# The first norm's weights as one row, spread over the partitions by two products

## The chip, the cores and the metric

The kernel runs on one core of a Trainium2 chip. The metric is the device time of one execution in microseconds (us). The kernel before takes 1307.15 us, the median of three runs (1306.59 to 1307.22).

## The reference

A decoder trunk with four pre-norm layers over 256 tokens of width 1024, in float32. Each layer is a token mixer (latent attention, block-sparse attention, a state-space scan, latent attention again) and then a squared-ReLU MLP. What matters here is the very beginning: every mixer starts from `rmsnorm(x, norm_mix[i])`, and the first one multiplies that by `mla_w_in`.

```
def rmsnorm(x, g):
    y = x * rsqrt(mean(x * x, axis=-1) + 1e-6)
    return y * g                      # g: 1024 weights, the same for all tokens

for i in range(4):
    h = rmsnorm(x, norm_mix[i])
    x = x + mixer_i(h)                # i = 0: proj = h @ mla_w_in, ...
    x = x + sq_relu_mlp(rmsnorm(x, norm_mlp[i]), w1[i], w2[i])
return rmsnorm(x, norm_final)
```

## The kernel before, in words

Tokens lie on the 128 partitions, so the 256 tokens are two tiles, t = 0 and t = 1, each 128 x 1024. The kernel is written with explicit semaphores; each engine has one program, in a fixed order, and waits where it needs something.

**A norm, stage 0.** ScalarE squares a tile and sums each row (line 621). VectorE makes mean plus epsilon (`ms`, line 697), GpSimd raises it to the power -0.5 (`rstd`, line 781, in `pool_norm`), and VectorE multiplies `x * rstd * gbc` in two halves of 512 columns (line 703, in `dve_scale_x`). `gbc` is a 128 x 1024 tile that holds the 1024 weights of the norm on every partition. TensorE turns each half by four transposes against the identity `ident` (line 797, `pe_tr`), ScalarE copies the result out of PSUM as the high part of a split into two numbers (line 649), and VectorE makes the low part (line 725).

**Weights.** All weight matrices come in `units` of up to 1 MB, in order, through four slots of `raw`. SyncE issues their loads (line 2214) between loads of other things; ScalarE makes the high part `whi` (lines 565 and 566), VectorE the low part `wlo` (lines 579 and 582), and a slot's next load waits for that. Units 0 and 1 are the two halves of the first 512 columns of `mla_w_in`, and they are split in halves so that TensorE can start early. Unit 2 is loaded by two DMAs (the last 64 columns of `mla_w_in`, and a part of `mla_w_uq`), unit 3 is from `mla_w_ukv`.

**The order in stage 0.** ScalarE: squares of tile 0, high parts of tile 0, `whi` of unit 0, squares of tile 1, high parts of tile 1, `whi` of unit 1, then unit 2. VectorE: `ms`, `xn` and low parts of tile 0, `wlo` of unit 0, `ms` of tile 1, four small rotary operations (`dve_turns`), `xn` and low parts of tile 1, nine more small ones (`dve_angles`), `wlo` of unit 1. TensorE: transposes of tile 0, seven products of `ident` with itself that nobody reads (line 2314), unit 0 with tile 0, transposes of tile 1, unit 0 with tile 1, unit 1 with tile 0, the small bias product (line 1673), unit 1 with tile 1, and then the rest of latent attention.

**SyncE's queue at the start:** x tile 0 (line 2194), `gbc` (line 2192, function `gains`, a load that reads the one row of weights 128 times), `ident` (line 2196), unit 0, x tile 1 (line 2200), unit 1 and so on.

**GpSimd's program at the start:** small memsets, loads of `pos_i` and `invf`, the power for tile 0, then loads of `relx` and `onehot` (for the bias product), two of `qkvg` for the first latent attention (`latent_gains(0)`, lines 2239 and 2241; they are read by VectorE at line 1500), then the power for tile 1, then a wait for unit 1's load, `latent_gains(1)` and seven small loads for the state-space layer (lines 2259 and 2260). Then come the powers of the latents (line 1557) and the store of the bias rows (line 1682).

Of the kernel before, what the change touches and what calls it, by code (L numbers as in the profile page):

```python
# [17 lines left out]
ALU = mybir.AluOpType  # L18
# [3 lines left out]
P = 128  # L22
SEQ = 256
T = SEQ // P
# [79 lines left out]
def build(nc, A, out, stages):  # L104

    ctx = ExitStack()
    with ctx:
        def sb(name, shape, dt=F32, c=ctx):
            return c.enter_context(nc.sbuf_tensor(name, shape, dt))

        def sem(name):
            return ctx.enter_context(nc.semaphore(name))
# [10 lines left out]
        gbc = sb("gbc", [P, DM])  # L123
# [10 lines left out]
        acc = [[ctx.enter_context(nc.psum_tensor(f"acc{t}{h}", [P, 512], F32)) for h in range(2)] for t in range(T)]  # L134
# [11 lines left out]
        x_loaded = [sem(f"x_loaded{t}") for t in range(T)]  # L146
        x_ready = sem("x_ready")
        gain_loaded = sem("gain_loaded")
        ssq_done = sem("ssq_done")
        ms_done = sem("ms_done")  # L150
        rstd_done = sem("rstd_done")
        xn_done = sem("xn_done")
# [51 lines left out]
        with ExitStack() as stage:  # L204
            S_sb = sb("S_sb", [P, 2, 384], F32, stage)
            P_sb = sb("P_sb", [P, 2, 384], F32, stage)
            PT_sb = sb("PT_sb", [P, 2, 384], F32, stage)
            ohi = sb("ohi", [P, 2, 2, SEQ], F32R, stage)
            olo = sb("olo", [P, 2, 2, SEQ], F32R, stage)
            qT = sb("qT", [P, 2, 4, SEQ], F32, stage)  # L210
            kT = sb("kT", [P, 2, 4, SEQ], F32, stage)
            v_sb = sb("v_sb", [P, 2, T, 512], F32, stage)
            with ExitStack() as mla:
                chi = sb("chi", [P, 4, SEQ], F32R, mla)
                clo = sb("clo", [P, 4, SEQ], F32R, mla)
                kpT = sb("kpT", [P, SEQ], F32, mla)
                qpT = sb("qpT", [P, 2, 2, SEQ], F32, mla)

                relx = sb("relx", [BUCKETS + 1, MOBA_H], F32, mla)
                onehot = sb("onehot", [BUCKETS + 1, 384], F32, mla)  # L220
                biasrow = sb("biasrow", [MOBA_H, 384], F32, mla)
                pos_i = sb("pos_i", [P, T], I32, mla)
                pos_f = sb("pos_f", [P, T], F32, mla)
                invf = sb("invf", [P, ROPE // 2], F32, mla)
                ang = sb("ang", [P, 4, T, ROPE // 2], F32, mla)
            bias = sb("bias", [P, MOBA_H, 384], F32, stage)
# [451 lines left out]
        def dve_scale_half(dve, j, t, half):  # L678

            n = slice(512 * half, 512 * half + 512)  # L680
            if j:
                dve.wait_ge(x_ready, (j - 1) * 2 * T + 2 * t + half + 1)
            else:
                dve.wait_ge(x_loaded[t], 16)
            dve.wait_ge(gain_loaded, 16 * (j + 1))
            nc.vector.tensor_tensor(xn[:, t, n], x[:, t, n], gbc[:, n], ALU.mult).then_inc(xn_done, 1)

        def dve_scale_x(dve, j, t, meanwhile=lambda: None):

            c = j * T + t  # L690
            if deferred(j):
                dve_scale_half(dve, j, t, 0)
                dve_scale_half(dve, j, t, 1)
                return
            wait_x(dve, j, t)
            dve.wait_ge(ssq_done, c + 1)
            nc.vector.tensor_scalar(ms[:, c:c + 1], ssq[:, c:c + 1], 1.0 / DM, EPS, ALU.mult, ALU.add).then_inc(ms_done, 1)
            meanwhile()
            dve.wait_ge(gain_loaded, 16 * (j + 1))
            dve.wait_ge(rstd_done, norm_index[j] * T + t + 1)  # L700
            for half in range(2):
                n = slice(512 * half, 512 * half + 512)
                nc.vector.scalar_tensor_tensor(out=xn[:, t, n], in0=x[:, t, n], scalar=rstd[:, c:c + 1],
                                               in1=gbc[:, n], op0=ALU.mult, op1=ALU.mult).then_inc(xn_done, 1)

        def dve_gain_upper(dve, j, t):
            dve.wait_ge(gain_loaded, 16 * (j + 1))
            wait_x(dve, j, t)
            n = slice(512, 1024)
            nc.vector.tensor_tensor(xn[:, t, n], x[:, t, n], gbc[:, n], ALU.mult).then_inc(xg_done, 1)  # L710
# [253 lines left out]
        norm_index, n_full = {}, 0  # L964
# [1214 lines left out]
        @block.sync  # L2179
        def _(sp):  # L2180

            def gains(j):
                if j >= NN:
                    return
                if j:
                    sp.wait_ge(xn_done, 2 * j * T)
                if j == NN - 1:
                    src = A["norm_final"].unsqueeze(0)
                else:
                    kind, L, _ = stages[j]  # L2190
                    src = A["norm_mlp" if kind == "mlp" else "norm_mix"][L:L + 1, :]
                sp.dma_start(gbc[:], src.to_broadcast([P, DM])).then_inc(gain_loaded, 16)

            sp.dma_start(x[:, 0, :], A["x"][0, tok(0), :]).then_inc(x_loaded[0], 16)
            gains(0)
            sp.dma_start(ident[:], A["c_ident"]).then_inc(ident_loaded, 16)
            for n, (a, b, srcs) in enumerate(units):
                s, k = n % SLOTS, n // SLOTS
                if n == 1:
                    sp.dma_start(x[:, 1, :], A["x"][0, tok(1), :]).then_inc(x_loaded[1], 16)  # L2200
                if n == SLOTS:
                    sp.dma_start(mask[:], A["c_mask"]).then_inc(mask_loaded, 16)
                if n in stage_unit:
                    gains(stage_unit[n] + 1)
                if k:
                    sp.wait_ge(w_split[s], k)
                w = b // len(srcs)
                for i, src in enumerate(srcs):
                    if isinstance(src, tuple):
                        off, k_rows, width, src = src  # L2210
                        dst = raw[:, s, off:off + k_rows * width].rearrange("p (a b) -> p a b", a=k_rows)
                    else:
                        dst = raw[:, s, :a * b].rearrange("p (a b) -> p a b", a=a)[:, :, i * w:(i + 1) * w]
                    sp.dma_start(dst, src).then_inc(raw_loaded[s], 16)
            for t in range(T):
                for half in range(2):
                    if half:
                        sp.wait_ge(xn_upper_done, norm_index[NN - 1] * T + t - T + 1)
                    else:
                        sp.wait_ge(xn_done, 2 * ((NN - 1) * T + t + 1))  # L2220
                    n = slice(512 * half, 512 * half + 512)
                    sp.dma_start(out[0, t * P:(t + 1) * P, n], xn[:, t, n]).then_inc(out_stored, 16)
            sp.wait_ge(out_stored, 32 * T)

        @block.gpsimd
        def _(pool):
# [3 lines left out]
            pool.wait_ge(pool_const, 2)  # L2230
            nc.gpsimd.memset(ones[:], 1.0).then_inc(pool_const, 1)
            pool.wait_ge(pool_const, 3)
            pool.dma_start(pos_i[:], A["positions"].rearrange("o (t p) -> p (o t)", p=P),
                           allow_slow_non_contiguous=True).then_inc(rope_loaded, 16)
            pool.dma_start(invf[:], A["c_invfreq"].to_broadcast([P, ROPE // 2])).then_inc(rope_loaded, 16)
# [2 lines left out]
            def latent_gains(i):  # L2238
# [2 lines left out]
                pool.dma_start(qkvg[:, i, QR:QR + KVR],  # L2241
                               A["mla_kv_norm"][i:i + 1, :].to_broadcast([P, KVR])).then_inc(qkvg_loaded[i], 16)

            pool.dma_start(relx[0:BUCKETS, :], A["rel_bias"]).then_inc(rel_loaded, 16)
            pool.dma_start(onehot[:], A["c_onehot"]).then_inc(rel_loaded, 16)
            latent_gains(0)
            if 0 in norm_index:
                pool_norm(pool, 0, [1])
            pool.wait_ge(raw_loaded[1], raw_count[1])
            latent_gains(1)  # L2250
            if "ssd" in kinds:
# [54 lines left out]

        @block.tensor
        def _(te):
            te.wait_ge(ident_loaded, 16)
            if "moba" in kinds and not bias_in_mla:  # L2310
                pe_bias(te)
            pe_tr(te, 0, 0)
            for _ in range(7):
                nc.tensor.matmul(acc[0][0][:, 0:P], ident[:], ident[:], start=True, stop=True)
            for j, (kind, L, i) in enumerate(stages):
                if kind == "mlp":
                    pe_mlp(te, j, L)
                if kind == "ssd":
                    pe_ssd(te, j, L)
                if kind == "mla":  # L2320
                    pe_mla(te, j, L)
                if kind == "moba":
                    pe_moba(te, j, L)
                if j + 1 < len(stages) and not deferred(j + 1):
                    pe_tr(te, j + 1, 0)
# [20 lines left out]
```

## Time and profile before

| what | value |
|---|---|
| median of 3 runs | 1307.15 us (1306.59 to 1307.22) |
| the profiled execution, its own time | 1307.72 us |
| its span, first to last instruction | 1305.9 us |
| TensorE busy with products | 1279.3 us, 98% of the span |
| VectorE busy | 891.4 us, 68% |
| ScalarE busy | 672.6 us, 51% |
| GpSimd busy | 43.5 us, 3% |

How to read it: times are microseconds from the start of the span. PE is TensorE's products and PEld its weight loads, DVE is VectorE, ACT ScalarE, POOL GpSimd and SPq SyncE's queue. L703 is line 703 of the kernel. A float32 product with float32 operands shows as two records in the trace. The ends of TensorE's records are modelled, and they overlap, so the distance between starts is the pace.

### The profile page before, as it was taken

How to read it: one execution, taken by the hardware profiler on the slowest of the kernel's cores; microseconds unless marked ns; L12 is line 12 of the kernel's file. 1: busy time of each engine (PE TensorE's matmuls, PEld its weight loads, DVE VectorE, ACT ScalarE, POOL GpSimd, SP SyncE). 2: the span in 40 equal slices, each digit the busy share in tenths (PEclk: the TensorE clock that was granted, in tenths of full speed). 3: DMA queues.
4: the chain of work that ended last, by engine and by line, in shares of the span. 5: the costliest groups of instructions: out<-in, count | busy, mean ns of one | idle time of the engine just before them, and what ended most of it. 6: DMA issues, size and time to landing. Idle time of an engine off the chain costs nothing.

```text
span 1305.9 us, 18369 instructions
## 1 busy us (share of the span) xinstructions
PE 1279.3 (98%) x7578; PEld 1118.2 (86%) x7578; DVE 891.4 (68%) x1180; ACT 672.6 (51%) x861; POOL 43.5 (3%) x58
## 2 busy tenths in 40 slices
PE   6999999999999999999999999999999999999998
PEld 5888888888999888887999888888887888888886
DVE  5877666665666666666899886766667876666664
ACT  5555554444555554444776654544445646454442
POOL 3000000000000000000101110000000000000000
PEclk9999999999999999999999999999999999999999
DMA  8754466555845375555574643755554334565540
GB/s 287 145 171 147 144 228 207 193 193 162 233 148 184 131 257 193 193 166 161 176 229 136 199 155 124 246 193 193 191 182 141 116 132 130 166 237 193 193 162 33
DMA packets 146067, 230.93 MB, mean 177 GB/s; under 512 B 7683, under 2 KB 112429, under 8 KB 145984
## 3 DMA queue, kind: packets, MB, share of 16 engines
q1 hardware_dynamic: 143136, 221.66, 51.0%
q0 software_dynamic: 2848, 8.10, 2.9%
q8 instruction: 61, 1.00, 0.3%
q14 instruction: 22, 0.18, 0.0%
HBM read 227.08 MB, written 2.65 MB: 176 GB/s over the span
## 4 chain that ended last, share of the span: by engine, by line
PE 83%; DVE 13%; DMA 1%; issue 1%; ACT 1%; POOL 1%; SPq 0%; POOLq 0%; DVEq 0%; ACTq 0%
PE bank L981 16%; PE acc L903 12%; PE acc L904 12%; PE acc L907 12%; PE bank L985 8%; PE bank L599 5%; PE bank L601 5%; PE bank L600 5%; DVE wlo L582 5%; DVE cacc L1961 2%; PE bank L1413 1%; PE bank L1116 1%; PE bank L797 1%; PE bank L1419 1%; PE bank L1101 1%
## 5 line engine op out<-in xcount | busy, mean ns | idle before, releaser
L582 DVE TENSOR_TENSOR wlo<-raw,whi 128x2048 fp32r<-128x2048 f32 (+2 forms) x207 | 464.8, 2255 | 139.9 <-ACT whi L566 139.8
L566 ACT ACTIVATE whi<-raw 128x2048 fp32r<-128x2048 f32 (+2 forms) x207 | 387.2, 1882 | 46.3 <-PE acc L907 44.1
L981 PE MATMUL bank<-hsplit,whi 128*128 128x512 f32 x896 | 219.1, 389 | 0.0
L904 PE MATMUL acc<-wlo,uhi 128*128 128x512 f32 x512 | 200.1, 391 | 0.0
L903 PE MATMUL acc<-whi,uhi 128*128 128x512 f32 x512 | 200.0, 391 | 0.0
L981 PEld LDWEIGHTS bank<-hsplit,whi 128*128 128x128 f32 x896 | 168.2, 188 | 34.8
L907 PE MATMUL acc<-whi,ulo 128*128 128x512 f32 x512 | 159.2, 390 | 0.0
L599 PE MATMUL bank<-hsplit,whi 128*128 128x256 f32 (+2 forms) x540 | 154.0, 285 | 0.5 <-DVE xn L1991 0.5
L601 PE MATMUL bank<-hsplit,wlo 128*128 128x256 f32 (+2 forms) x540 | 150.9, 279 | 0.0
L600 PE MATMUL bank<-hsplit,whi 128*128 128x256 f32 (+2 forms) x540 | 150.8, 279 | 0.0
L1038 ACT ACTIVATE relu<-bank 128x512 f32<-128x512 f32 x56 | 33.5, 598 | 183.8 <-PE bank L985 183.8
L985 PE MATMUL bank<-hsplit,wlo 128*128 128x256 f32 x896 | 120.3, 277 | 0.0
L985 PEld LDWEIGHTS bank<-hsplit,wlo 128*128 128x128 f32 x896 | 114.3, 188 | 4.7
L907 PEld LDWEIGHTS acc<-whi,ulo 128*128 128x128 f32 x512 | 96.1, 188 | 20.4
L903 PEld LDWEIGHTS acc<-whi,uhi 128*128 128x128 f32 x512 | 96.1, 188 | 18.6
L904 PEld LDWEIGHTS acc<-wlo,uhi 128*128 128x128 f32 x512 | 96.1, 188 | 18.2
L599 PEld LDWEIGHTS bank<-hsplit,whi 128*128 128x128 f32 (+2 forms) x540 | 100.7, 186 | 1.8 <-issue 1.4
L600 PEld LDWEIGHTS bank<-hsplit,whi 128*128 128x128 f32 (+2 forms) x540 | 101.0, 187 | 0.9 <-issue 0.7
L601 PEld LDWEIGHTS bank<-hsplit,wlo 128*128 128x128 f32 (+2 forms) x540 | 101.2, 187 | 0.0
L1059 DVE TENSOR_TENSOR relu<-bank,relu 128x512 f32<-128x512 f32 x56 | 38.7, 691 | 91.1 <-ACT relu L1038 91.1
L1043 ACT ACTIVATE uhi<-rsq 128x512 fp32r<-128x512 f32 x64 | 40.6, 634 | 111.2 <-DVE rsq L1061 82.2
L1064 DVE TENSOR_TENSOR ulo<-rsq,uhi 128x512 fp32r<-128x512 f32 x64 | 44.3, 692 | 47.7 <-ACT uhi L1043 47.7
(252 smaller groups left out, 1811.9 us busy)
## 6 DMA issues: line engine op xcount, KB each, us to landing
raw<-in_mlp_w SPq DMA_DIRECT2D x128, 1024.0 KB, 5.5
raw<-in_ssd_w_in SPq DMA_DIRECT2D x18, 1024.0 KB, 5.4
raw<-in_mla_w_o SPq DMA_DIRECT2D x16, 1024.0 KB, 4.9
raw<-in_mla_w_ukv SPq DMA_DIRECT2D x8, 1024.0 KB, 6.0
raw<-in_moba_w_qkv SPq DMA_DIRECT2D x16, 512.0 KB, 5.4
raw<-in_ssd_w_out SPq DMA_DIRECT2D x8, 1024.0 KB, 5.6
raw<-in_mla_w_uq SPq DMA_DIRECT2D x8, 768.0 KB, 5.8
raw<-in_mla_w_in SPq DMA_DIRECT2D x4, 1024.0 KB, 7.4
```

What stands on the lines that cost most here:

```text
L566: nc.scalar.activation(high[:, lo:e], raw[:, s, lo:e], ACT.Copy).then_inc(w_hi_done[s], 1)
L582: nc.vector.tensor_tensor(low[:, lo:e], raw[:, s, lo:e], high[:, lo:e].bitcast(F32), ALU.subtract).then_inc(w_split[s], 1)
L599: nc.tensor.matmul(ps, lhs[0], rhs[0], start=start, stop=False)
L600: nc.tensor.matmul(ps, lhs[0], rhs[1], start=False, stop=False)
L601: return nc.tensor.matmul(ps, lhs[1], rhs[0], start=False, stop=stop)
L903: nc.tensor.matmul(acc[t][half][:], lh, wh[:, k, n], start=begin and k == 0, stop=False)
L904: nc.tensor.matmul(acc[t][half][:], lh, wl[:, k, n], start=False, stop=False)
L907: mm = nc.tensor.matmul(acc[t][half][:], ll, wh[:, k, n], start=False, stop=end and k == 1)
L981: nc.tensor.matmul(ps, w[0][:, k, m * P:(m + 1) * P], hsplit[:, k].rearrange("p a n -> p (a n)"), start=k == 0, stop=False)
L985: return nc.tensor.matmul(ps[:, 0:SEQ], w[1][:, k, m * P:(m + 1) * P], hsplit[:, k, 0, :], start=False, stop=k == KD - 1)
L1043: nc.scalar.activation(uhi[:, c % 2].rearrange("p a b -> p (a b)"), rsq[:, c % 2, :], ACT.Copy).then_inc(uhi_done, 1)
L1064: nc.vector.tensor_tensor(ulo[:, c % 2].rearrange("p a b -> p (a b)"), rsq[:, c % 2, :], uhi[:, c % 2].rearrange("p a b -> p (a b)").bitca ...
```

## The change

One row of weights (4 KB) is loaded into partition 0 of `gbc` instead of the copy for all 128 partitions. GpSimd sets 128 ones in partition 0 of a buffer that is free then. TensorE multiplies the column of ones (1 x 128) with each half of the row (1 x 512), which leaves the weights on every partition in the two PSUM tiles `acc[1][0]` and `acc[1][1]`; VectorE reads them from there in line 703, for both tiles. All later norms load `gbc` as before; their counts are one load lower. In GpSimd's program the power of tile 1 moves ahead of the loads of `relx`, `onehot` and the first pair of `qkvg`.

```diff
+            ones_row = S_sb[0:1, 0, 0:P]
@@ dve_scale_x
-            dve.wait_ge(gain_loaded, 16 * (j + 1))
+            if j:
+                dve.wait_ge(gain_loaded, 16 * j)
+            else:
+                dve.wait_ge(gains_spread, 1)
             dve.wait_ge(rstd_done, norm_index[j] * T + t + 1)
             for half in range(2):
                 n = slice(512 * half, 512 * half + 512)
                 nc.vector.scalar_tensor_tensor(out=xn[:, t, n], in0=x[:, t, n], scalar=rstd[:, c:c + 1],
-                                               in1=gbc[:, n], op0=ALU.mult, op1=ALU.mult).then_inc(xn_done, 1)
+                                               in1=gbc[:, n] if j else acc[1][half][:], op0=ALU.mult,
+                                               op1=ALU.mult).then_inc(xn_done, 1)
@@ SyncE
             sp.dma_start(x[:, 0, :], A["x"][0, tok(0), :]).then_inc(x_loaded[0], 16)
-            gains(0)
+            sp.dma_start(gbc[0:1, :], A["norm_mix"][0:1, :]).then_inc(gain_row_loaded, 16)
             sp.dma_start(ident[:], A["c_ident"]).then_inc(ident_loaded, 16)
@@ GpSimd
             nc.gpsimd.memset(ones[:], 1.0).then_inc(pool_const, 1)
             pool.wait_ge(pool_const, 3)
+            nc.gpsimd.memset(ones_row, 1.0).then_inc(ones_row_set, 1)
             pool.dma_start(pos_i[:], ...
...
+            if 0 in norm_index:
+                pool_norm(pool, 0, [1])
             pool.dma_start(relx[0:BUCKETS, :], A["rel_bias"]).then_inc(rel_loaded, 16)
             pool.dma_start(onehot[:], A["c_onehot"]).then_inc(rel_loaded, 16)
             latent_gains(0)
-            if 0 in norm_index:
-                pool_norm(pool, 0, [1])
             pool.wait_ge(raw_loaded[1], raw_count[1])
             latent_gains(1)
@@ TensorE
+            te.wait_ge(ones_row_set, 1)
+            te.wait_ge(gain_row_loaded, 16)
+            for half in range(2):
+                mm = nc.tensor.matmul(acc[1][half][:], ones_row, gbc[0:1, 512 * half:512 * half + 512], start=True, stop=True)
+            mm.then_inc(gains_spread, 1)
             te.wait_ge(ident_loaded, 16)
```

## Rows read from the trace of the kernel before

**Rows 1.** The page's chain that ended last: shares of the span by engine.

```profile
PE 83%; DVE 13%; DMA 1%; issue 1%; ACT 1%; POOL 1%; SPq 0%; POOLq 0%; DVEq 0%; ACTq 0%
```

**Rows 2.** The same chain in order, first 30 us: start, length, what.

```profile
2.12 9.68 DMA raw<-in_mla_w_in
...
11.82 1.07 ACT whi L565
...
12.91 1.23 DVE wlo L579
14.14 1.03 DVE wlo L582
...
19.32 0.47 PE bank L599
...
25.03 0.75 PE bank L1673 x2
...
26.28 2.27 DVE wlo L582
```

**Rows 3.** Timeline of tile 0: start, length, engine, line, [idle before, releaser].

```profile
0.75 0.38 SPq L2194 DMA_DIRECT2D x<-in_x  x1
1.19 0.42 SPq L2192 DMA_DIRECT2D gbc<-in_norm_mix  x1
...
4.89 1.06 ACT L621 ACTIVATE junk<-x 128x1024 f32<-128x1024 f32 x1 [2.87 <-DMA x<-in_x]
...
7.06 1.41 DVE L703 SCALAR_TENSOR_TENSOR xn<-x,rstd,gbc 128x512 f32<-128x512 f32 x2 [0.75 <-POOL rstd L781]
...
7.96 1.94 PE L797 MATMUL bank<-ident,xn 128*128 128x128 f32 x8 [7.96 <-DVE xn L703]
...
9.69 2.86 PE L2314 MATMUL acc<-ident 128*128 128x128 f32 x14
...
9.93 0.60 ACT L649 ACTIVATE hsplit<-bank 128x512 fp32r<-128x512 f32 x1 [0.26 <-PE bank L797]
...
11.82 1.06 ACT L565 ACTIVATE whi<-raw 128x1024 fp32r<-128x1024 f32 x1 [1.29 <-DMA raw<-in_mla_w_in]
```

**Rows 4.** DMA issues of the first 40 us: issues, KB, median us from issue to landing.

```profile
x<-in_x SPq DMA_DIRECT2D x2, 512.0 KB, 7.7
...
gbc<-in_norm_mix SPq DMA_DIRECT2D x1, 512.0 KB, 5.1
...
qkvg<-in_mla_kv_norm POOLq DMA_DIRECT2D x2, 128.0 KB, 6.8
...
ident<-in_c_ident SPq DMA_DIRECT2D x1, 64.0 KB, 5.0
...
onehot<-in_c_onehot POOLq DMA_DIRECT2D x1, 49.5 KB, 5.6
...
drow<-in_ssd_d POOLq DMA_DIRECT2D x1, 0.1 KB, 3.4
```

**Rows 5.** TensorE's records of line 2314: duration ns min, median, max.

```profile
L2314 PE MATMUL acc<-ident x14: 275/421/422, 9.7 to 12.3; 128*128 128x128 f32 x14
```

**Rows 6.** Windows: busy us (records) of PE, PEld, DVE, ACT, POOL; granted clock, DMA share, GB/s.

```profile
5.00:10.00 5.00, 2.04 (x10) 2.07 (x11) 1.86 (x4) 1.71 (x4) 2.75 (x5) 1.00 0.94 295
```

**Rows 7.** Timeline of tile 1's norm and GpSimd's next loads, same columns as rows 3.

```profile
15.45 0.56 POOL L781 TENSOR_TENSOR rstd<-ms,neghalf 128x1 f32<-128x1 f32 x1 [6.31 <-DVE ms L697]
...
16.36 1.41 DVE L703 SCALAR_TENSOR_TENSOR xn<-x,rstd,gbc 128x512 f32<-128x512 f32 x2
...
17.86 1.26 ACT L649 ACTIVATE hsplit<-bank 128x512 fp32r<-128x512 f32 x2 [2.75 <-PE bank L797]
...
19.31 0.58 POOL L2239 DMA_DIRECT2D qkvg<-in_mla_q_norm  x1 [3.29 <-DMA raw<-in_mla_w_in]
```

**Rows 8.** VectorE by line and shape: count, busy us, mean ns, idle before.

```profile
L957 DVE SCALAR_TENSOR_TENSOR x<-acc,rstd,x 128x512 f32<-128x512 f32 x16 | 11.4, 746 | 6.0 <-PE acc L907 6.0
...
L703 DVE SCALAR_TENSOR_TENSOR xn<-x,rstd,gbc 128x512 f32<-128x512 f32 x4 | 2.8, 748 | 0.8 <-POOL rstd L781 0.8
```

More of the change, by code:

```diff
@@ L148, in build @@
         gain_loaded = sem("gain_loaded")
+        gain_row_loaded = sem("gain_row_loaded")
+        ones_row_set = sem("ones_row_set")
+        gains_spread = sem("gains_spread")
         ssq_done = sem("ssq_done")
@@ L698, in dve_scale_x @@
             meanwhile()
-            dve.wait_ge(gain_loaded, 16 * (j + 1))
+            if j:
+                dve.wait_ge(gain_loaded, 16 * j)
+            else:
+                dve.wait_ge(gains_spread, 1)
             dve.wait_ge(rstd_done, norm_index[j] * T + t + 1)
@@ L703, in dve_scale_x @@
                 nc.vector.scalar_tensor_tensor(out=xn[:, t, n], in0=x[:, t, n], scalar=rstd[:, c:c + 1],
-                                               in1=gbc[:, n], op0=ALU.mult, op1=ALU.mult).then_inc(xn_done, 1)
+                                               in1=gbc[:, n] if j else acc[1][half][:], op0=ALU.mult,
+                                               op1=ALU.mult).then_inc(xn_done, 1)
         def dve_gain_upper(dve, j, t):
-            dve.wait_ge(gain_loaded, 16 * (j + 1))
+            dve.wait_ge(gain_loaded, 16 * j)
             wait_x(dve, j, t)
@@ L2184, in gains @@
                     return
-                if j:
-                    sp.wait_ge(xn_done, 2 * j * T)
+                sp.wait_ge(xn_done, 2 * j * T)
                 if j == NN - 1:
```

## The prediction

> **What bounds the kernel now.** I read the page's chain first. It lies on TensorE for 83% of the span and on VectorE for 13%, with only 1% on DMA [rows 1]. So the change can touch only the start, and what it moves there is kept or lost once. The chain in order of time shows the start [rows 2]: until 11.80 us it is the load of weight unit 0 (issued 2.12, 9.68 us long), then ScalarE's high parts at 11.82, VectorE's low parts at 12.91 and 14.14, then tile 1's norm, and TensorE from 19.32 nearly without a pause to the bias product at 25.03. None of the later steps waits for a load in this chain. If `whi` of unit 0 starts D earlier, all of this moves by D, and behind it the kernel is bound by engines and keeps it.
>
> The timeline of tile 0 shows the second strand [rows 3]. x lands before 4.89, `xn` starts at 7.06, the transposes at 7.96, ScalarE's last high part at 9.93, and it ends at 10.53. ScalarE then idles 1.29 us for unit 0. Tile 0's norm therefore has a slack of 1.29 us, and this is the most that loads alone can give unless tile 0 gets faster too.
>
> **The load that goes.** `gbc` lands at 1.19 + 5.1 = 6.3 us, x at 4.85, both of 512 KB and one behind the other in one queue [rows 3, 4]. The copy thus holds the queue back some 6.3 - 4.9 = 1.4 us. Unit 0 should land at 11.8 - 1.4 = 10.4. The GpSimd loads that move away from 7 to 9 us are 50 + 128 + 128 KB, about 0.3 MB; at 295 GB/s [rows 6] that is another 1.0 us at most. Unit 0 lands between 9.4 and 10.4, which is at or ahead of ScalarE's 10.53. Weights stop being the late one, and tile 0 decides.
>
> **What is put into tile 0's strand.** `xn` used to wait for `rstd` at 7.06. It now waits also for two products, and these for the row. Three terms:
>
> 1. The row's landing. It is issued behind x at 1.19. If it stays behind x it lands just after 4.85; I take 4.9. The bounds: the smallest load of the stretch took 3.4 us (0.1 KB, another queue), so 4.6; `ident`, issued third and 64 KB, took 5.0, so 6.2 [rows 3, 4].
> 2. The products, 4 x 128 columns each in float32. Line 2314 shows seven of 128 columns in 2.86 us, 0.41 us each [rows 3], so 4 x 0.41 = 1.63 us for one of 512 and 3.3 for two. The upper limit goes by the slow records alone: they overlap by half of 421 ns [rows 5], so 0.42 per product of 128 and 3.4 for two. That is the pace of 1.2 GHz, although the page's granted clock reads 1.00 there [rows 6]: within the same line the records fall from 421 to 275 ns [rows 5], and later the 384-column bias product takes 0.75 us [rows 2], which is 1.0 for 512 columns and 2.0 for two. So 2.0 at the fast level, 3.4 at the slow one. TensorE has done nothing before, as before its first transposes; I take 3.4. The end of the last record trails by 0.2 (421 less half).
> 3. From `xn` to ScalarE free: 10.53 - 7.06 = 3.47 us in tile 0, with slow transposes. Tile 1 does the same from 16.36 to 17.86 + 1.26 = 19.12, 2.76 us, at the fast level [rows 7]. So 3.5 or 2.8.
>
> Sum at the slow level: 4.9 + 3.4 + 0.2 + 0.05 for the wait + 3.47 = 12.0, against 11.82 before: 0.2 us later. If the clock has risen when the transposes run (before, TensorE worked from 7.96 on and its records became short at about 12; now it works from 4.9, with a pause of about 1 us behind the products): 4.9 + 3.4 + 0.2 + 0.05 + 2.76 = 11.3, 0.5 us earlier. I take the middle, 11.65, so D = 0.15 us.
>
> A rule of the Trainium skill speaks against the hope in the second sum: "TensorE: Matmul & The Clock Gate", "Part 1: The HAM clock gate", says the array starts at 1.2 GHz, is let up only after sustained work and falls back when idle. By it a product issued first always pays the slow pace, and the pause for `xn` may put the rise off; the sum would be 12.0. The records of line 2314 agree with the start [rows 5]; no row shows a pause of this kind.
>
> **The rest of the change, at nothing.** VectorE reads the weights from PSUM: the same operation with a PSUM operand took 746 ns against 748 from SBUF [rows 8]. The memset is GpSimd's, over long before the row lands; it puts `pos_i` off by under 0.2 us, and that is wanted in `dve_turns` only after 15.2. `ident` comes earlier. The seven idle products follow the transposes as before, and unit 0's products with tile 0 have a reserve of about a microsecond ahead of tile 1's transposes; if that cover is gone, see the fourth case. The `acc` tiles are not wanted before the first output products, tens of us later.
>
> The power of tile 1 stays where it is (15.45, released by `ms` [rows 7]), because GpSimd had long issued its loads. What moves is behind it: `relx`, `onehot` and the two `qkvg` are now issued from about 16.0 in steps of 0.56, so `onehot` at about 16.6, landing after its 5.6 us at 22.2 [rows 4], wanted by the bias product at 25.03 [rows 2]; 2.8 us of cover. The last `qkvg` is issued at 17.7 and lands after 6.8 at 24.5 (median; 1 to 2 us more in a full queue), wanted behind the `wlo` that ends at 28.55 [rows 2, 4]. `latent_gains(1)` started at 19.31 behind unit 1's landing [rows 7]; GpSimd is free at 18.2, and the eight issues behind it end no later than before. With the counts of loads shifted by one, nothing else on SyncE's queue changes.
>
> The profiled execution: 1307.72 us for a span of 1305.9, so 1.8 lie around the span. With D = 0.15 it would be 1307.57. The median of the runs is 0.57 below the profiled one, hence 1307.0.
>
> **The rivals.**
>
> *The relief comes through.* The row or the clock is kinder than I take them, and unit 0's load is again what ScalarE waits for, at 9.4 to 10.4. The time is 1307.15 - 1.4 = 1305.75, at the utmost 1307.15 - 2.4 = 1304.75. For it: at the fast level throughout the sum is 4.9 + 2.0 + 0.2 + 2.8 = 9.9. Against it: line 2314's slow records at just this point. The same end is reached if the row lands by 3.3. The Trainium skill gives a small load a fixed cost near 2 us ("DMA: Bandwidth & Descriptors", "Anatomy of one DMA"), which by an estimate from that page would be 3.2; no load in these rows took under 3.4, and all stood in full queues.
>
> *The row is late: slower.* The new wait takes the place of the one removed. Each microsecond of the row's landing past 4.65 (slow transposes: 11.82 - 7.15 = 4.65) is lost one for one, because VectorE has nothing to do meanwhile and ScalarE, TensorE and the `whi` of unit 0 are all queued behind it. At `ident`'s 6.2 it is 1.5 us: 1308.7. Against it: 4 KB behind x has hardly a reason to be 1.3 us later than x.
>
> *The clock stays low past 14 us: slower.* The pause for `xn` starts the rise anew. The transposes of tile 0 then end at 11.5, the idle products at 14.4, and the 12 products of unit 0 with tile 0 run at 0.43 instead of 0.23 us: to 19.6, when tile 1's transposes are wanted at 17.2. Price 2.4, with the 0.2 from above 2.6: 1309.8. Against it: from 9.5 on TensorE has the same work without a stop as it had from 7.96 before, and there the records were short by 12.3 [rows 5].
>
> *The change doesn't do what it says*, because the queue was held up by x and not by `gbc`; unit 0 still lands near 11.8. Then tile 0's strand, at 11.3 to 12.0, hides beside it, and the time is 1307.2. It can't be told from my forecast by time, only by ScalarE's idle before line 565.
>
> **How the numbers follow.** Tile 0 decides, with ScalarE free at 11.2 to 12.2: 1306.5 to 1307.6, chance 0.62. Relief comes through: 1305.75, 0.18. Row late: 1308.2 to 1308.7, 0.10. Clock low: up to 1309.8, 0.04. Unit 0 not earlier: 0.06. The range of 8 in 10 takes the first case, most of the relief and half of the late row: 1305.3 to 1308.4. What can be told from no change is 0.2%, 2.6 us. No case on the faster side reaches 1304.5, the best being 1304.75; I leave 0.03 for what I don't see. On the slower side the low clock just reaches 1309.8, and loads moved into a fuller stretch could add to it: 0.04. Same: 0.93.
>
> **What would show it.** In the changed kernel: line 703 first at about 8.6 instead of 7.06, released by the products; the two products from about 4.9, four records over 3.4 us; ScalarE's `whi` at 11.3 to 12.0 with its wait on ScalarE's own high parts and none on a load; unit 0 landed by 10.4; tile 1's first product at 19.2. The forecast is wrong if line 565 starts before 11 (then row or clock), if the bias product waits for its loads, or if the span moves by more than line 565 does.

## The result and the profile after

The changed kernel takes 1310.01 us (median of 12 runs, 1308.41 to 1312.27). The kernel before, over 12 runs with the three of the forecast among them: 1307.8 us (1306.06 to 1311.27). The ratio is 1.0019, interval 1.0011 to 1.0026: slower by 2.5 us by the ratio, by 2.2 us between the medians. The forecast was 1307.0, within 1305.3 to 1308.4, with a chance of 0.93 for no change above 0.2%.

The profiled execution has a span of 1309.1 us, 3.2 more than before. Its chain in order (start, length, what) answers to [rows 2]:

```profile
1.94 11.79 DMA raw<-in_mla_w_in
...
13.75 1.06 ACT whi L569
...
14.84 1.23 DVE wlo L583
16.07 0.79 DVE wlo L586
...
21.23 0.47 PE bank L603
...
26.95 0.75 PE bank L1681 x2
...
28.20 2.27 DVE wlo L586
...
32.43 2.67 POOL c_rstd L1565
...
36.71 0.65 PE bank L603
37.36 0.43 PE bank L604
37.79 0.43 PE bank L605
```

The load of unit 0 now ends at 13.73 instead of 11.80. Everything behind it is later by the same 1.9 us: `whi` 13.75 for 11.82, TensorE 21.23 for 19.32, the bias product 26.95 for 25.03 [rows 2]. That is the first part of the loss. The second is in the last three lines: products of 512 columns start 0.43 us apart, where those of the head (13 to 30 us) start 0.23 apart. The windows of the two profiles show TensorE's granted clock there (columns as in [rows 6]), the changed kernel first:

```profile
34.00:36.00 2.00, 0.39 (x4) 0.13 (x2) 1.41 (x4) 0.54 (x2) 2.00 (x2) 1.00 1.16 380
36.00:42.00 6.00, 5.95 (x29) 4.61 (x29) 2.91 (x11) 3.07 (x4) 0.16 (x1) 0.72 0.75 208
```

The kernel before:

```profile
36.00:42.00 6.00, 5.88 (x47) 5.26 (x46) 4.65 (x19) 4.60 (x5) 0.00 (x0) 1.00 0.62 124
```

TensorE was idle for most of 34 to 36 us (0.39 us busy), waiting for the power of the latents, and then worked at the lower of its two levels, 1.2 GHz, for a part of the next window (0.72 on average). The lower level cost 1.5 us in this execution (1.9 us behind the first profile at 28 us, 3.4 at 44, by TensorE's records). The pause itself is no longer than before, 1.66 us in both. Whether the change causes it is asked below.

The timeline of tile 0 in the changed kernel answers to [rows 3]:

```profile
4.36 1.06 ACT L625 ACTIVATE junk<-x 128x1024 f32<-128x1024 f32 x1 [2.33 <-DMA x<-in_x]
...
4.64 3.75 PE L2320 MATMUL acc<-gbc,S_sb 1*128 1x512 f32 x4 [4.64 <-DMA gbc<-in_norm_mix]
...
8.43 1.41 DVE L710 SCALAR_TENSOR_TENSOR xn<-x,rstd,acc 128x512 f32<-128x512 f32 x2 [2.65 <-PE acc L2320]
9.32 1.94 PE L805 MATMUL bank<-ident,xn 128*128 128x128 f32 x8 [0.93 <-DVE xn L710]
...
11.30 0.60 ACT L653 ACTIVATE hsplit<-bank 128x512 fp32r<-128x512 f32 x1 [0.26 <-PE bank L805]
...
13.75 1.06 ACT L569 ACTIVATE whi<-raw 128x1024 fp32r<-128x1024 f32 x1 [1.85 <-DMA raw<-in_mla_w_in]
```

The reader is to see two things. The strand of tile 0 came out near the sum at the slow level: row at 4.64, products 3.75 us, `xn` at 8.43, ScalarE free at 11.90. And ScalarE then still idled 1.85 us for unit 0, more than the 1.29 of before. What the page shows for DMA from 4 to 8 us is in the last column of these windows (GB/s; before it the share of DMA). After:

```profile
4.00:8.00 4.00, 3.35 (x4) 1.16 (x4) 0.15 (x1) 1.15 (x2) 0.57 (x1) 1.00 0.51 126
8.00:12.00 4.00, 3.07 (x14) 2.71 (x14) 2.17 (x4) 1.20 (x2) 0.00 (x0) 1.00 0.98 317
```

Before:

```profile
4.00:8.00 4.00, 0.04 (x1) 0.07 (x2) 1.09 (x3) 1.15 (x2) 1.61 (x3) 1.00 0.94 247
8.00:12.00 4.00, 4.00 (x19) 4.00 (x20) 1.86 (x3) 1.38 (x3) 1.14 (x3) 1.00 1.02 388
```

With less to load, the engines of DMA were busy for 51% of that stretch instead of 94%. The difference in bytes, (247 - 126) x 4 = 0.48 MB, is about the copy that was taken away (0.52 MB). All else, taken together, moved as slowly as before.

### The profile page after: what moved, and what is told of

Read it like the earlier page. It is cut to its first block, busy times and chain, and to the rows that moved or that the text cites. A ratio compares the mean times of both kernels' runs of the same rounds, so it can differ in the third digit from the quotient of the medians.

```text
span 1309.1 us, 18379 instructions
## 1 busy us (share of the span) xinstructions
PE 1284.6 (98%) x7582; PEld 1120.6 (86%) x7582; DVE 891.4 (68%) x1180; ACT 671.6 (51%) x861; POOL 43.6 (3%) x59
## 4 chain that ended last, share of the span: by engine, by line
PE 90%; DVE 6%; issue 1%; ACT 1%; DMA 1%; POOL 0%; SPq 0%; POOLq 0%; DVEq 0%; ACTq 0%
PE bank L989 16%; PE acc L911 12%; PE acc L912 12%; PE acc L915 12%; PE bank L993 8%; PE bank L603 7%; PE bank L605 7%; PE bank L604 7%; DVE wlo L586 2%; PE bank L1421 1%; PE bank L1124 1%; PE bank L1758 1%; DMA raw<-in_mla_w_in 1%; PE bank L805 1%; PE bank L1427 1%
```

## The experiments

Theory A: the start's loads differ so much between executions that one profile says nothing. Theory B or L: without the copy, unit 0 lands later. Rivals: the order of GpSimd's loads (C), the two products (P). Each kernel has 11 or 12 runs and one profile. In the table, "landed" is unit 0, "GB/s" the rate from 4 to 8 us, "taken" the start of ScalarE's first `whi`, in that profile. row_nopos, row_noinvf, row_nosmall and copy_nosmall have zeros for inputs of the rotary angles, and row_noproducts leaves out the norm's weights.

| kernel | ratio to before, interval | landed | GB/s | taken |
|---|---|---|---|---|
| before, first profile | | 11.8 | 247 | 11.82 |
| before_again | 1.0003 (0.9994 to 1.0012) | 11.6 | 229 | 11.66 |
| pool_only | 0.9998 (0.9989 to 1.0006) | 11.1 | 267 | 11.11 |
| copy_products | 0.9996 (0.9987 to 1.0005) | 11.0 | 228 | 12.02 |
| changed, first profile | 1.0019 (1.0011 to 1.0026) | 13.7 | 126 | 13.75 |
| after_again | 1.0010 (1.0001 to 1.0019) | 11.7 | 137 | 11.73 |
| row_only | 1.0008 (0.9999 to 1.0018) | 13.1 | 133 | 13.15 |
| row_noproducts | 1.0003 (0.9994 to 1.0012) | 12.8 | 145 | 12.82 |
| row_filler | 1.0012 (1.0000 to 1.0023) | 12.3 | 138 | 12.37 |
| row_nopos | 1.0004 (0.9993 to 1.0015) | 12.4 | 151 | 12.45 |
| row_noinvf | 0.9999 (0.9990 to 1.0007) | 10.3 | 189 | 12.12 |
| row_nosmall | 1.0010 (1.0000 to 1.0019) | 9.6 | 267 | 11.83 |
| copy_nosmall | 0.9985 (0.9977 to 0.9994) | 9.7 | 285 | 9.93 |
| row_late_halves | 0.9995 (0.9986 to 1.0004) | 9.7 | 288 | 10.89 |
| copy_late | 0.9990 (0.9981 to 0.9998) | 9.5 | 291 | 10.41 |
| copy_late_again | 0.9983 (0.9973 to 0.9993) | 9.5 | 298 | 10.53 |

**The two kernels again.** No edit.

> The kernel before, unchanged, to see how much of the profile's start repeats. Theory A (the load of unit 0 is slow in the first 9 us by itself, and how slow differs from one execution to the next): unit 0 lands anywhere from 11.5 to 14 us, and need not be the 11.80 of the first profile. Theory B (taking the copy away makes the load of unit 0 later): it lands at 11.8 +- 0.2 again. Both: ratio 1.000.

> The changed kernel, unchanged. Theory A: unit 0 lands anywhere from 11.5 to 14 us, and the time is above before only by what tile 0's norm costs and by the clock that fell at 36.8 us. Theory B: 13.7 +- 0.2 again. Ratio 1.001 to 1.003 in both. If the clock's fall at 36.8 us is a matter of phase, it may be absent in this profile.

The landing does vary (11.7 in one execution of the changed kernel, 13.7 in another), the rate from 4 to 8 us hardly (247 and 229 against 126 and 137). So theory A holds for the landing and falls for the rate, and theory B's 13.7 for the repeat was missed. The clock also fell in the kernel before:

```profile
36.00:42.00 6.00, 6.00 (x39) 5.24 (x38) 3.69 (x17) 3.78 (x3) 0.00 (x0) 0.76 0.67 136
```

Its span was 1307.6 us with unit 0 at 11.6. Matched record by record, TensorE is 0.2 us earlier than in the first profile of before at 28 us and 1.25 later at 44. Over all runs the mean clock is alike: 0.9964 and 0.9969 for the changed kernel, 0.9968 for 33 runs of before. So the change is not needed for the fall. Whether it makes it likelier is not settled: the windows from 33 to 42 us show it in 8 of the 16 profiles, in 6 of the 9 with the products and in 2 of the 7 without. Three others show a fall between 14 and 26 us (row_noproducts, row_filler, copy_late_again). The 11 or 12 runs of a kernel spread over 2.3 to 5.6 us, which hides small effects; single runs show mean clocks from 0.994 to 0.999, and 0.001 of 1308 us is 1.3 us.

**The two halves of the change apart.** row_only is the changed kernel with GpSimd's loads in the old order, pool_only has the copy and only the new order. The edit of pool_only:

```diff
+            if 0 in norm_index:
+                pool_norm(pool, 0, [1])
             pool.dma_start(relx[0:BUCKETS, :], A["rel_bias"]).then_inc(rel_loaded, 16)
             pool.dma_start(onehot[:], A["c_onehot"]).then_inc(rel_loaded, 16)
             latent_gains(0)
-            if 0 in norm_index:
-                pool_norm(pool, 0, [1])
```

> Only the row and the two products; GpSimd's loads in the old order. Theory B: like the changed kernel, unit 0 at 13.5 to 13.9, ratio 1.0015 to 1.002. Rival C (the order of GpSimd's loads does it): like before, unit 0 at 10.5 to 11.8, tile 0's norm late, ratio 1.0000 to 1.0005. Line 710 first at 8.4 in both.

> Only the new order of GpSimd's loads; weights copied to all partitions as before. Theory B: unit 0 at 11.0 to 11.8, ratio 0.9993 to 1.000. Rival C: unit 0 at 13.5 or later, ratio 1.0015 to 1.002.

Rival C falls: the new order alone shows 267 GB/s and unit 0 at 11.1. The row alone has the low rate (133 GB/s) and unit 0 at 13.1, a little before theory B's 13.5 to 13.9. Its ratio, 1.0008, was to be 1.0015 at least, and its interval holds 1.

**Loads or products.** row_noproducts multiplies by ones; copy_products loads the copy as well:

```diff
-            for half in range(2):
-                mm = nc.tensor.matmul(acc[1][half][:], ones_row, ...)
+            nc.vector.memset(gbc[:], 1.0).then_inc(gains_spread, 1)
```

> The row is loaded, but no product spreads it; the first norm multiplies by ones instead of its weights (that factor is left out). Tile 0's norm is then as early as x allows. Theory P (the two products are what costs): line 710 first at 6.5, ratio 0.9990 to 1.0000. Theory L (the loads cost: without the copy, unit 0 lands later, at 11.7 to 13.7 us against 11.1 to 11.8): ScalarE's first high part of unit 0 at 12 to 13.7 although tile 0 is ready at 10.0; ratio 1.0003 to 1.0010.

```diff
+            sp.dma_start(gain_row, A["norm_mix"][0:1, :]).then_inc(gain_row_loaded, 16)
+            sp.dma_start(gbc[:], A["norm_mix"][0:1, :].to_broadcast([P, DM])).then_inc(copy_loaded, 16)
```

> The changed kernel with the copy for all partitions loaded as well (unread), behind the row; the row goes to another buffer. Theory P: like the changed kernel, ratio 1.0008 to 1.0019. Theory L: unit 0 at 11.1 to 11.9 again, tile 0's norm done at about 11.9 beside it, ratio 0.9998 to 1.0005.

In its profile row_noproducts had tile 0 ready at 10.0 and ScalarE idle for 2.81 us, waiting for unit 0:

```profile
12.82 1.06 ACT L570 ACTIVATE whi<-raw 128x1024 fp32r<-128x1024 f32 x1 [2.81 <-DMA raw<-in_mla_w_in]
```

So the load is late without any product in the kernel. copy_products was not slower at all; there unit 0 was down at 11.0 and tile 0 decided, at 12.02. By their profiles this is theory L; by their times alone, both intervals hold 1, and neither share can be sized.

**The two small loads.** The packet records show those of `invf` (16 of 1024 bytes) taking 0.46 us each on average in the kernel before and 0.72 in the changed one (0.38 and 0.56 in the repeats). row_nosmall and copy_nosmall do without `invf` and `pos_i`:

```diff
-            pool.dma_start(pos_i[:], ...).then_inc(rope_loaded, 16)
-            pool.dma_start(invf[:], ...).then_inc(rope_loaded, 16)
+            nc.gpsimd.memset(pos_i[:], 0).then_inc(rope_loaded, 16)
+            nc.gpsimd.memset(invf[:], 0.0).then_inc(rope_loaded, 16)
```

> The changed kernel without GpSimd's loads of pos_i and invf (memsets to zero in their place; the rotary angles are left out). Their 32 packets took 0.2 to 1.0 us each between 3 and 10 us. Theory L1 (these packets hold the engines' queues up, and without the copy they meet the weights' stream instead): unit 0 lands by 10.5, ScalarE takes it at 11.9 when tile 0 is done; ratio 0.9998 to 1.0004. Theory L2 (the weights' first read is slow by itself): unit 0 still at 11.7 to 13.7, GB/s between 4 and 8 us still under 200.

> The kernel before without the same two loads. Theory L1: unit 0 lands 0.5 to 1.5 us sooner, at 10.3 to 11.2; ratio 0.9990 to 0.9997. Theory L2: unit 0 at 11.1 to 11.8, ratio 1.000.

This is the widest step of the study. 17 KB less, and unit 0 lands at 9.6 to 9.7 in both, with the copy and without. The kernel with the copy gains 0.15%, for ScalarE takes the unit as soon as tile 0 lets it:

```profile
9.93 1.05 ACT L565 ACTIVATE whi<-raw 128x1024 fp32r<-128x1024 f32 x1
```

In row_nosmall tile 0 lets it at 11.83 only:

```profile
4.68 3.75 PE L2319 MATMUL acc<-gbc,S_sb 1*128 1x512 f32 x4 [4.68 <-DMA gbc<-in_norm_mix]
...
8.46 1.41 DVE L710 SCALAR_TENSOR_TENSOR xn<-x,rstd,acc 128x512 f32<-128x512 f32 x2 [2.53 <-PE acc L2319]
...
11.83 1.05 ACT L569 ACTIVATE whi<-raw 128x1024 fp32r<-128x1024 f32 x1
```

With the loads out of the way, the products cost what they delay `xn` by: 11.83 - 9.93 = 1.9 us, and the times differ by as much or more (1.0010 against 0.9985, 2.7 us between the medians). Both expectations for the time were missed. The miss of row_nosmall matters: unit 0 no longer holds it up, its `whi` starts where that of before did in the first profile (11.82), and it is still as slow as the repeat of the changed kernel (1.0010 both; 0.9998 to 1.0004 had been expected). The two loads one at a time, each from the changed kernel:

> The changed kernel without the load of invf (zeros in its place; the rotary angles are left out). Its 16 packets of 1024 bytes took 0.7 to 1.0 us each. If invf is what holds the weights up: unit 0 lands by 10.5, ScalarE takes it at 11.85, ratio 1.0000 to 1.0010 as without both. If it is pos_i: 11.7 to 13.7.

> The changed kernel without the load of pos_i (zeros in its place; the rotary angles are left out). If pos_i (16 packets of 64 bytes, 0.2 to 0.8 us each, and its 256 elements of 4 bytes) is what holds the weights up: unit 0 lands by 10.5. If it is invf: 11.7 to 13.7.

Without `invf` unit 0 lands at 10.3, without `pos_i` at 12.4, which is inside the 11.7 to 13.7 of the kernels with both. So `invf` does most of it; for a part of `pos_i` only the step from 10.3 to 9.6 speaks, one profile each. The 0.7 to 1.0 us per packet of the expectation is too narrow: in the changed kernel `invf`'s took 0.05 to 1.5 us.

**The loads moved, not removed.** They are issued behind the power of tile 0, and VectorE's four small operations move behind `xn` of tile 1. The power of tile 1 moves ahead of the other loads as in pool_only (not shown again here):

```diff
             if 0 in norm_index:
                 pool_norm(pool, 0, [0])
+            pool.dma_start(pos_i[:], ...).then_inc(rope_loaded, 16)
+            pool.dma_start(invf[:], ...).then_inc(rope_loaded, 16)
...
-                dve_scale_x(dve, j, 1, lambda: dve_turns(dve))
+                dve_scale_x(dve, j, 1)
+                dve_turns(dve)
```

> The kernel before (the copy stays), with GpSimd's order changed: power of tile 0, then the loads of pos_i and invf, then the power of tile 1, then the rest; VectorE's dve_turns moves behind the xn of tile 1, so that these two loads have time. Theory L1 (the small packets of these two loads hold up the weights between 3 and 10 us): the packets move to 8 to 13 us, unit 0 lands at 9.7 to 10.7 us, ScalarE takes it at 10.0 to 10.7; ratio 0.9985 to 0.9993. Theory L2 (any small load does it, wherever it is): unit 0 at 11.1 to 11.8, ratio 1.000.

> The copy with the late small loads once more, on another chip or at another time: unit 0 at 9.4 to 10.4, ratio 0.9985 to 0.9995.

This is the version that beats both kernels: 0.9990 and 0.9983, by these ratios 1.3 and 2.2 us faster than before. The load rate and ScalarE's `whi` in its two profiles are alike. The window of the first, with 291 GB/s:

```profile
4.00:8.00 4.00, 0.06 (x1) 0.09 (x2) 1.11 (x3) 1.15 (x2) 1.60 (x3) 1.00 0.94 291
```

And its timeline, where `pos_i` is issued at 6.92 and is there when VectorE reads it at 15.99:

```profile
6.92 0.88 POOL L2236 DMA_DIRECT2D pos_i<-in_positions  x1
...
10.41 1.05 ACT L565 ACTIVATE whi<-raw 128x1024 fp32r<-128x1024 f32 x1
...
15.99 0.17 DVE L2150 CAST pos_f<-pos_i 128x2 f32<-128x2 int32 x1
```

The same with the row, and with one wait per product so that the first half of `xn` starts at 6.81:

```diff
+                if not j:
+                    dve.wait_ge(gains_spread, half + 1)
```

> The changed kernel with the same late loads, and with VectorE waiting for one product per half instead of both. L1: unit 0 lands by 10.5; line 710 first at 6.7, its second half at 8.4, ScalarE takes unit 0 at 11.0 to 11.3 when tile 0 is done; ratio 0.9990 to 0.9998. If only the wait for both products mattered: unit 0 still at 11.7 to 13.7 and ratio over 1.0005.

ScalarE takes unit 0 at 10.89; the ratio 0.9995 holds 1 in its interval. The second half of `xn` still waits until 8.44 for its product, which is why the row does not reach the copy's 10.41 and 10.53 there.

**Is it any 512 KB, or this copy?** row_filler loads 128 different rows of x where the copy stood:

```diff
+            sp.dma_start(v_sb[:, 0, :, :].rearrange("p t n -> p (t n)"), A["x"][0, tok(1), :]).then_inc(filler_loaded, 16)
```

> The changed kernel with a plain load of 512 KB, from 128 different rows of x, in the place where the copy stood, into a buffer that nobody reads. Theory F (what protects the weights is any 512 KB ahead of them, so that the small packets meet something else): unit 0 at 11.0 to 12.0, the small queue's share between 2 and 12 us 2.6 to 6%, ratio 1.0000 to 1.0008. Theory G (it is the copy's own kind, one source row read 128 times, that is kind to the small packets): unit 0 at 12.5 to 14, small queue's share 7 to 12%, ratio 1.001 to 1.002.

These are bytes and shares of the two queues from 2 to 12 us (packets, MB, share of 16 engines). With the copy and the new order, pool_only:

```profile
q1 hardware_dynamic: 1367, 3.19, 92.0%
q0 software_dynamic: 64, 0.02, 5.1%
```

The changed kernel:

```profile
q1 hardware_dynamic: 1069, 2.27, 65.0%
q0 software_dynamic: 64, 0.02, 9.8%
```

With the filler:

```profile
q1 hardware_dynamic: 1101, 2.62, 74.1%
q0 software_dynamic: 64, 0.02, 9.5%
```

The share of these 64 small packets is 5.1% with the copy and 2.6% in copy_products; without it 9.8, 7.3 in the repeat and 9.9 in row_noproducts; with the filler 9.5. The filler's rate from 4 to 8 us is 138 GB/s. Theory F is out, for the rate and for the small packets. The landing, 12.3, lies between the two theories' numbers. What it is in the copy that leaves room (one source row read 128 times) is argued, not shown; the filler also goes to another buffer, and TensorE waits for it.

**Did the copy hold unit 0 back at all?** The trace has sixteen landing events for this load, and ScalarE waits for the last. In the kernel before they come from 9.13 to 11.80 us (mean of the eighth and ninth 9.48), in its repeat from 9.10 to 11.63 (9.66). In the changed kernel they come from 8.06 to 13.73 (11.62), in its repeat from 7.90 to 11.68 (10.03). So the first parts did gain over 1 us, and the middle and the last did not. Without the small loads the middle gains as well, 8.2 in row_nosmall for 9.3 in copy_nosmall, and the last part is at 9.63 for 9.71. Even there the last part, which is what counts, gains 0.1 us from 0.5 MB less ahead of it. What holds the last parts then is open.

## Why the prediction was wrong

- **The relief by the copy: the step that failed.** I put unit 0 at 11.8 - 1.4 = 10.4, less up to 1.0 for GpSimd's moved loads. Measured without the copy: 11.7 to 13.7 in four profiles that keep the two early small loads, against 11.0 to 11.8 in four with the copy; without the small loads 9.6 against 9.7. So the relief is 0.1 us at best, not 1.4. I had taken a byte for a byte in one queue and one landing for the whole load. The first of its sixteen parts did come over 1 us sooner, but the last one decides, and with the small loads in the stretch it came at about the old time or later. From 4 to 8 us the copy moved beside loads that were slow without it too. Its end 1.4 us behind x said when the copy was done, not what it kept others from. A hint stood in the rows, 295 GB/s from 5 to 10 us [rows 6], against the 388 from 8 to 12 us shown above; but the share of DMA, 0.94, looked full.
- **The rival that unit 0 would not land earlier** got 0.06 and was taken to end at 1307.2. The case that it would land later was not among the rivals.
- **The row's landing**: 4.9 forecast, 4.64 measured, 4.58 in the repeat and 4.72 in row_only. x itself came 0.5 us sooner. The early landing by 3.3 that one rival needed did not come. In the rival of the late row the strand is 7.15 long; its terms add up to 7.12, which changes nothing.
- **The products**: 3.4 + 0.2 forecast, 3.75 measured. They went at the pace of the lower level throughout (2.0 for two had been the price at the higher), and so did the transposes behind them (1.94 us, as before), though the granted clock of these windows reads 1.00. The rule of the Trainium skill ("TensorE: Matmul & The Clock Gate", "Part 1: The HAM clock gate"), by which the sum would be 12.0, was the better guide here. The trace agrees: of 12.0 and 11.3, 11.90 came, and my middle of 11.65 was too early by 0.25.
- **Tile 0 decides**: only where the loads let it. In row_nosmall, with unit 0 at 9.6, it does, at 11.83 against the 12.0 of the sum at the slow level. There the whole mechanism that I described can be seen, and it gives no gain: 1.0010.
- **The edits put at nothing** were at nothing: VectorE's `xn` from PSUM took 1.41 us for two, as from SBUF; the bias product found its loads; the order alone gave 0.9998.
- **The clock.** I had it as a rival at one place (behind the products), where it did not happen in either profile of the changed kernel. It fell at 36.8 us in the profiled execution and near there in one of two of the kernel before, so the change is not needed for it. The base moved too: my 1307.15 was the median of three runs, and the 12 gave 1307.8.
- **The time.** 2.2 us between the medians; the repeat gives 1.0010 (1.4 us between the medians there). In the 13 profiles in which the clock kept its higher level from 14 to 26 us, TensorE at 28 us is off from the first profile of before by what "taken" is off, within 0.25 us. So the start costs what it delays ScalarE's first `whi`; what single executions gain or lose behind 44 us is not followed here. Two things delay it. The profiles show a late unit 0 (taken at 12.9 on average over the changed kernel twice, row_only and row_noproducts, against 11.7 in the two profiles of before: 1.1 us), and tile 0's strand as a floor (ScalarE is free for the unit at 11.7 to 12.1 in the changed kernel twice, row_nosmall and row_noinvf, and at 9.9 to 10.7 where the copy stands and no product is made). How the loss divides is open. row_nosmall pays the floor alone and is at 1.0010; row_noproducts pays the late unit alone and is at 1.0003; the intervals overlap. The times lean to the floor more than the profiles do. For that to fit, the kernel before would often have to take unit 0 sooner than 11.7, as pool_only did (11.11), and one or two profiles do not tell.

## What to carry to other kernels

Do not price the bytes ahead of a load as its delay before something shows it: here 0.5 MB less brought the first parts forward and the last one, for which the kernel waits, by 0.1 us at most. Look at GB/s of the stretch, and where it dips (247 against 388 here, at a share of 0.94), look for small packets in it. Before spreading a row by products at a kernel's start, count them at TensorE's lower level, here 1.9 us for 512 float32 columns (3.75 for two). And a few small loads that nobody needs for 10 us are worth trying behind the first weights: 0.10 and 0.17% here.

## What the runs showed of the hardware

- Two loads of 17 KB in all, issued by GpSimd at 1.4 and 2.2 us, cost the load of the first weights 1.3 to 2.1 us (unit 0 at 9.7 without them, 11.0 to 11.8 with them beside the copy), and 2 to 4 us without the copy.
- The same 16 KB load of `invf` took 5.7 to 7.5 us to land in four profiles with the copy, and 7.6 to 9.4 in four without it (7.4 with the filler). The slowest, in the changed kernel:

```profile
invf<-in_c_invfreq POOLq DMA_DIRECT2D x1, 16.0 KB, 9.4
```

- 512 KB read from one row 128 times went through beside a stretch that otherwise moved 126 to 145 GB/s; 512 KB from 128 rows did not (138 GB/s in all).
- A load of 1 MB lands in sixteen parts, and these can be far apart: 8.06 to 13.73 us in the changed kernel, 9.04 to 9.54 in copy_late.
- TensorE's granted clock fell to 1.2 GHz in one execution of the kernel before and not in another, behind the same pause of 1.66 us (it ends at 33.93 and 34.14 us), at a cost of 1.5 us.
